# RWKV-7 block of a hybrid trunk: triangular inverse in 32x32 tiles, two chains in flight, tanh in place of sigmoid

## The reference, cut to what matters

```
def wkv_scan(r, w, k, v, a, b, s0, reverse):
    def step(S, xs):
        sa = einsum('bhvk,bhk->bhv', S, a_t)
        S = S * w_t + sa x b_t + v_t x k_t            # x: outer product
        return S, einsum('bhvk,bhk->bhv', S, r_t)

kk = normalised(kf * rw_kk)
for d in (forward, backward):
    w_log = -softplus(-(w0[d] + tanh(x_w) @ w2[d])) - 0.5
    decay = exp(-exp(w_log))                          # = exp(-exp(-0.5) * sigmoid(...))
    a_rate = sigmoid(a0[d] + x_a @ a2[d])
    k_d = kf * (1 + (a_rate - 1) * rw_ka)
    o_d, s_d = wkv_scan(rf, decay, k_d, vf, -kk, kk * a_rate, s0, reverse=d)
```

## Time and profile before

| | |
|---|---|
| median of three runs | 3419.12 us (3416.22 to 3426.52) |
| the profiled execution | 3412.67 us, its span 3410.9 us |
| mean granted TensorE clock | 0.929 of full speed |
| busy, whole span | PE 2957.4 us (87%), PEld 1759.9 (52%), DVE 1448.0 (42%), ACT 564.5 (17%), POOL 377.9 (11%) |
| `block_rwkv` | about 1030 to 1817 us of the span |
| HBM traffic in it | 22 GB/s, against 400 in the experts |

### The profile page before, as it was taken

One profiled execution on the slowest core, in us unless ns is written; L12 is line 12 of the kernel. 1 busy time (PEld: TensorE's weight loads), 2 busy tenths in 40 slices (PEclk: granted clock), 3 DMA queues, 4 the chain that ended last, 5 costly groups with the idle time before them and its releaser, 6 DMA issues. The chain is left out here.

```text
span 3410.9 us, 72845 instructions
## 1 busy us (share of the span) xinstructions
PE 2957.4 (87%) x32237; PEld 1759.9 (52%) x32237; DVE 1448.0 (42%) x2634; ACT 564.5 (17%) x1331; POOL 377.9 (11%) x431
## 2 busy tenths in 40 slices
PE   5899999998595888888884499977999999999993
PEld 1566666665375888888882245442333333323230
DVE  1677577663363665565652311142232232132123
ACT  2100000000352333333332311110000000000001
POOL 0100000000154232322211000000000000000000
PEclk8899999999597999999995799978999999999996
DMA  9565645552451000000005387777999999999997
GB/s 412 195 213 175 208 176 183 208 196 84 143 132 46 24 5 26 26 26 26 25 8 229 138 300 289 276 308 283 395 410 393 412 412 395 399 397 400 408 419 309
DMA packets 224486, 776.86 MB, mean 228 GB/s; under 512 B 55171, under 2 KB 119386, under 8 KB 155635
## 3 DMA queue, kind: packets, MB, share of 16 engines
q1 hardware_dynamic: 212626, 712.26, 54.1%
q0 software_dynamic: 11248, 60.87, 5.9%
q10 hardware_dynamic: 368, 0.10, 0.0%
HBM read 710.98 MB, written 62.18 MB: 227 GB/s over the span
## 5 line engine op out<-in xcount | busy, mean ns | idle before, releaser
L2068 PE MATMUL ex_ps<-experts_ring,ex_xe 128*32 128x512 f32 (+1 forms) x4608 | 674.6, 599 | 49.1 <-DMA experts_ring<-in_w_up 27.6
L2070 PE MATMUL ex_ps<-experts_ring,ex_xe 128*32 128x512 f32 (+1 forms) x1536 | 674.1, 599 | 0.0
L2068 PEld LDWEIGHTS ex_ps<-experts_ring,ex_xe 128*32 128x32 f32 (+1 forms) x4608 | 212.6, 107 | 497.0 <-issue 479.4
L474 DVE SCALAR_TENSOR_TENSOR pj_macc<-pj_mring,head_cond_t,pj_macc 128x1024 f32<-128x1024 f32 x240 | 296.9, 1277 | 184.0 <-DMA pj_mring<-in_w_ada 184.0
L2083 PE MATMUL ex_ps<-experts_ring,ex_hidt 128*32 128x512 f32 (+1 forms) x2304 | 334.3, 594 | 6.9 <-DVE ex_hidt L2150 6.9
L2085 PE MATMUL ex_ps<-experts_ring,ex_hidt 128*32 128x512 f32 (+1 forms) x768 | 333.8, 594 | 0.0
L547 PE MATMUL pj_ps<-head_hT,head_ring_in 128*128 128x320 f32 x1104 | 313.7, 437 | 5.9 <-DVE head_hT L447 3.5
L1866 PE MATMUL om_ps<-experts_ring,om_ot 128*128 128x512 f32 x640 | 287.1, 610 | 15.4 <-DMA om_ot<-scratch_o 15.4
L2172 DVE SCALAR_TENSOR_TENSOR ex_hid<-ex_hid,ex_gcol,ex_ps 80x512 f32<-80x512 f32 x16 | 11.9, 744 | 591.3 <-ACT ex_hid L2115 591.3
L547 PEld LDWEIGHTS pj_ps<-head_hT,head_ring_in 128*128 128x128 f32 x1104 | 211.4, 192 | 96.6 <-DVE head_hT L447 6.3
L2083 PEld LDWEIGHTS ex_ps<-experts_ring,ex_hidt 128*32 128x32 f32 (+1 forms) x2304 | 106.8, 106 | 225.9 <-issue 218.1
(11 more groups left out here) (357 smaller groups left out, 4417.4 us busy)
## 6 DMA issues: line engine op xcount, KB each, us to landing
experts_ring<-in_w_gate SPq DMA_DIRECT2D x128, 1024.0 KB, 21.9
experts_ring<-in_w_up SPq DMA_DIRECT2D x128, 1024.0 KB, 22.6
experts_ring<-in_w_down SPq DMA_DIRECT2D x128, 1024.0 KB, 21.3
experts_ring<-in_w_out SPq DMA_DIRECT2D x68, 1024.0 KB, 6.9
pj_mring<-in_w_ada SPq DMA_DIRECT2D x64, 1024.0 KB, 9.0
head_ring_in<-in_w_in SPq DMA_DIRECT2D x23, 2048.0 KB, 8.0
ada_ring<-in_w_ada SPq DMA_DIRECT2D x16, 2048.0 KB, 19.0
scratch_z<-pj_stage POOLq DMA_DIRECT2D x19, 640.0 KB, 8.2
```

Of the source, the lines that this page charges most:

```text
L474: a = nc.vector.scalar_tensor_tensor(acc, w, scalar, acc, ALU.mult, ALU.add)
L2068: pe.matmul(ps[rows, bank, :], xe[:, k, rows], cols, start=(k == 0), stop=(k == KD - 1))
L2070: mm = pe.matmul(ps[96:96 + rows.stop - rows.start, bank, :], xe[:, k, rows], up[:, g1], start=(k == 0), stop=(k == KD - 1))
```

## The change

It rewrites the order and the inverse inside `block_rwkv` and nothing else.

- The inverse is made only in 32x32 tiles: four levels (blocks of 2 to 16) on the two diagonal 32x32 tiles of each 64x64, that is on the four tiles (0,0), (1,1), (2,2), (3,3) of the array for the two heads, and a fifth level that fills the off-diagonal tile. `tt` has 32 columns; its transpose is no longer made by products (`dt`, `ti` go) but by VectorE's 32x32 transpose (`turn`). Batches are two, of five chunks. The result is spread into `tw` (64 columns) by GpSimd (`spread_own`) and by VectorE at the last level.
- Two chains run at a time, of the two directions, each in its own PSUM banks: in line u the second half of unit u-2's chain is interleaved stage by stage with the first half of unit u-1's. R goes from 6 to 4 banks. The state is scaled by one product with a decay pair that GpSimd forms (`decay_pairs`), in place of two pointer operands.
- Both sigmoids become tanh with scale 0.5 on ScalarE; the "1 +" is added by VectorE ahead of the scan, and `LAM` and the vectors are halved. `bb` = (rate + 1) times kk is formed by VectorE (`removal`) instead of GpSimd.
- The order in a line changes: `sc` first, with `w` and `a` of the next unit between; `bk`, `vt`, `s0` are fillers between the levels. `vt` is done once for a pair and not once for a unit, reads `vt` without ScalarE's copy, and `wa2`, `sin`, `bk` have two buffers. Masks are built for four 32-row groups.

The core of the diff ("..." where lines are left out):

```diff
-    LAM = float(np.exp(-0.5))
-    LEVELS = [2, 4, 8, 16, 32]
-    BATCH = [(0, 4), (4, 7), (7, 10)]
-    R = 6
...
+    LAM = 0.5 * float(np.exp(-0.5))
+    CHAINS = 2
+    R = 4
+    NS = 1 + CHAINS
+    HB, BC = CK // 2, NCK // 2
+    LAST_LV = 4
+    GROUPS = tuple(slice(HB * g, HB * g + HB) for g in range(4))
...
+    def plan(u):
+        fr = front_jobs(u + 1) + [None] * 5
+        vt = [("vt", b, u) for b in range(2)] if u % 2 == 0 else [None] * 2
+        items = [("sc", 0, u), fr[0], ("sc", 1, u), fr[1], ("sc", 2, u), fr[2], ("sc", 3, u), fr[3], ("sc", 4, u)]
+        items += ["scan"] if more else []
+        fill = [("bk", 0, u), ("bk", 1, u), ("bk", 2, u), fr[4], vt[0], vt[1]]
+        for lv in range(LAST_LV + 1):
+            for b in range(2):
+                items += (["turn%d" % b] if lv == 0 else []) + [("x", b, lv, u)]
+            if lv < 3:
+                items.append(fill[2 * lv])
+            if more and lv == 2:
+                items.append("removal")
+            for b in range(2):
+                items.append(("d", b, lv, u))
+                if more and lv == 3:
+                    items.append(("exp_in", "exp_inv")[b])
+                if more and lv == 4:
+                    items += (["pad_b"], ["pad_k", "pad_a"])[b]
+            if lv < 3:
+                items.append(fill[2 * lv + 1])
+            if more and lv == 3:
+                items += ["exp_ex", "decay"]
...
+    def sequence(u):
+        old, new = chain(u - 2, BC, NCK), chain(u - 1, 0, BC)
+        return [s for pair in itertools.zip_longest(old, new) for s in pair if s is not None]
+    COST = {"sc": 9, "w": 6, "a": 6, "s0": 2, "bk": 9, "vt": 6, "x": 7, "d": 7}
...
         @block.gpsimd
-            for i in range(6):
-                n = 2 ** i
-                for rows in HEADS:
+            for i in range(5):
+                n = 2 ** i
+                for rows in GROUPS:
...
+            def start(u, b):
+                n = MADE + 3 * (2 * u + b)
+                pool.wait_ge(dve_ev, RANK[G["sc", (BC * b + BC - 1) // 2, u]])
+                nc.gpsimd.tensor_tensor(part[:], lt, first[:].unsqueeze(1).to_broadcast([P, BC, 2, HB]), ALU.mult).then_inc(tinit, 1)
...
         @block.tensor
-                elif kind == "ti":
-                    pe.wait_ge(tinit, 6 * u + 2 * b + 2)
...
+                    last = key[2] == LAST_LV
+                    for i in range(BC):
+                        c = BC * b + i
+                        out = bank[:, i * HB:(i + 1) * HB]
+                        for g, rows in enumerate(GROUPS):
+                            at = GROUPS[g ^ 1] if last else rows
+                            if kind == "x":
+                                h = (g + 1) % 2 if last else g % 2
+                                lhs, rhs = sc[rows, u % NS, c, 0, HB * h:HB * h + HB], tm[rows, c, :]
+                            else:
+                                lhs, rhs = xm[rows, c, :], tt[rows, c, :]
+                            mm = pe.matmul(out[at], lhs, rhs, start=True, stop=True)
...
         @block.scalar
-                    return nc.scalar.activation(sg[:, cols], bank[:, 0:HALF], ACT.Sigmoid, bias=pp[:, 5 + d:6 + d])
+                    a = nc.scalar.activation(sg[:, cols], bank[:, 0:HALF], ACT.Tanh, scale=0.5, bias=pp[:, 5 + u % 2:6 + u % 2])
...
         @block.vector
-            dve.wait_ge(once_in, 64)
-            dve.wait_ge(made, 2)
+            dve.wait_ge(once_in, 8 * 16)
+            dve.wait_ge(tinit, MADE)
+            def turn(u, b):
+                nc.vector.transpose(chunks(tm, b).rearrange("p c k -> p (c k)"), chunks(tt, b).rearrange("p c k -> p (c k)")).then_inc(turned, 1)
...
+            def scan(v):
+                nc.vector.tensor_scalar(sg[:], sg[:], 1.0, None, ALU.add).then_inc(cs_done, 1)
                 nc.vector.tensor_tensor_scan(cs[:], reset[:], sg[:], 0.0, ALU.mult, ALU.add).then_inc(cs_done, 1)
+            def removal(v):
+                nc.vector.scalar_tensor_tensor(bb[:], ar[:], 1.0, kk[:], ALU.add, ALU.mult).then_inc(cs_done, 1)
```

More of the change, by code:

```diff
@@ L1106, in block_rwkv, with on_act @@
+    LINES = [timeline(u) for u in range(NU + CHAINS)]
+    JOBS = front_jobs(0) + [i for line in LINES for i in line if not isinstance(i, str) and i[0] != "seq"]
+    G = {key: g for g, key in enumerate(JOBS)}
+    def on_act(key):
+        return key[0] in ("w", "a", "s0", "vt", "bk") or key[0:1] + key[2:3] == ("x", LAST_LV)
+    RANK = [sum(on_act(m) == on_act(key) for m in JOBS[:g + 1]) + on_act(key) for g, key in enumerate(JOBS)]
     with ExitStack() as ctx:
@@ L1147, in block_rwkv @@
-        w_done, w_ev, u_done, u_ev, z_done, z_ev, o_ev, s_ready = (sem(n) for n in ("wd", "we", "ud", "ue", "zd", "ze", "oe", "sr"))
-        fs_done, fo_out, osum_done, o_out = sem("fs"), sem("foout"), sem("osum"), sem("oout")
-        block = ctx.enter_context(nc.Block())
-        NLOAD = 10 * 16
-        def periods(period):
-            for p in range(NPAIR):
-                for d in range(2):
-                    period(p, d, first=p + d == 0, last=p == NPAIR - 1 and d == 1)
+        par_ready = sem("parrdy")
@@ new lines, in _ @@
+            pool.wait_ge(once_in, 8 * 16)
+            front(0)
+            scaled_r(0)
+            decay_pairs(0)
+            added = 0
+            for u in range(NU):
+                for b in range(2):
+                    start(u, b)
+                if u + 1 < NU:
+                    front(u + 1)
+                    scaled_r(u + 1)
+                for b in range(2):
+                    spread_own(u, b)
+                if u + 1 < NU:
+                    decay_pairs(u + 1)
+                if u % 2 == 0 and u // 2 >= CHAINS:
+                    add_directions(added)
+                    added += 1
@@ L1366, in stage @@
[L1366 to L1370 removed]
+                        emptied([("x", 1, LAST_LV, v), ("d", 1, LAST_LV, v)])
@@ L1379, in period @@
-            def period(p, d, first, last):
-                for item in timeline:
-                    if item[0] == "job":
-                        run_job(item[1], p, d, first, last)
-                    elif not first:
-                        stage(item[1], item[2], 2 * p + d - 1, 1 - d)
-            pe.wait_ge(loads, NLOAD)
-            for n, (kind, half) in enumerate(FRONT_JOBS):
-                front_job(kind, half, 0, rot[:, n]).then_inc(job, 1)
-            periods(period)
-            for i, s in stages:
-                stage(i, s, 2 * NPAIR - 1, 1)
+                    pe.wait_ge(w_ev[k], q + 1)
@@ L1406, in empty @@
[L1406 to L1418 removed]
+            act.wait_ge(once_in, 8 * 16)
@@ L1483, in _ @@
-            copy_values(0)
-            act.wait_ge(par_ready, 2)
-            for n, (kind, half) in enumerate(FRONT_JOBS):
-                act.wait_ge(job, n + 1)
-                take_front(kind, half, 0, rot[:, n]).then_inc(act_ev, 1)
-            exponentials(0, 0, first=True)
-            periods(period)
-            for i, s in stages:
-                stage(i, s, 2 * NPAIR - 1, 1, NPAIR - 1)
+                    act.wait_ge(u_done[k], q + 1)
+                    nc.scalar.copy(usb[:, k, :], wu[:, k, DH:2 * DH]).then_inc(u_ev[k], 1)
+                else:
+                    act.wait_ge(z_done[k], q + 1)
+                    act.wait_ge(z_ev[k], q + 2)
+                    if i == 0 and v // 2:
+                        act.wait_ge(osum_done, v // 2)
+                    nc.scalar.copy(of[:, v % 4, c * CK:(c + 1) * CK], zo[:, k, DH:2 * DH]).then_inc(o_ev[k], 1)
@@ L1583, in _ @@
-            vectors(0)
-            scan(FRONT)
-            scaled(0, 0, first=True)
-            scaled(1, 0, first=True)
-            scaled_a(0, 0, ready=False)
-            periods(period)
-            for i, s in stages:
-                stage(i, s, 2 * NPAIR - 1, 1)
+                    nx = ORDER[k][i + 1]
+                    nc.vector.tensor_tensor(fs[:, k, :], tmp[:, k, :], ec[:, r, c:c + 1].to_broadcast([P, DH]), ALU.mult)
+                    nc.vector.tensor_tensor(st[:, k, :], s0[:, r, :], ec[:, r, nx:nx + 1].to_broadcast([P, DH]), ALU.mult).then_inc(s_ready[k], 1)
+                elif i + 1 < NCK:
+                    nc.vector.tensor_tensor(st[:, k, :], tmp[:, k, :], ecp[:, r, c:c + 1].to_broadcast([P, DH]), ALU.mult).then_inc(s_ready[k], 1)
```

611 lines of the change are left out of this document (311 added, 300 removed).

## The result

The changed kernel takes 3534.23 us (median of 4 runs, 3525.01 to 3541.05) against 3419.67 for the kernel before (3416.22 to 3426.52): 1.033 times as long, interval 1.030 to 1.036. It is slower, where I had forecast 3383 us, and it lies above my range, too. The profiled execution took 3541.05 us with a span of 3539.3, 128.4 us over that of before.

What follows compares the result with a forecast made beforehand. TensorE and its waits were taken as the bound: a period falls from 45.8 to 43.0 us, fifteen give -42, the start adds 6, so 3377 us profiled and 3383 median, range 3300 to 3480.

Steps and rivals of the forecast that it cites:

- Price of a record: Inverse's 800 records on 32x32 tiles: 11 ns each, 8.8 us a period, ends 5.8 to 23.4.
- issue bound: Rival: inverse's records still cost 29.2 ns, the pace of issue; period 51 us, kernel 3505 us; chance 0.11.
- paced between: Rival: inverse's records cost 22 ns, between 15 and 29.2; period 48.0 us, kernel 3458 us; chance 0.07.
- Change of shape: TensorE switching between 32x32 and other tiles, 36 to 38 times a period: 0.1 us each, 3.7 us, ends 0 and 4.5.
- Gaps: Two new TensorE waits a period: 2.9 us ahead of the first x, 2.5 ahead of the next unit's first sc.
- Chain's waits: Waits for the chain's stage results, some 5 us a period, all go with two chains in flight.
- Clock: Half-clock dips in the recurrence: 1.5 a period at 1.8 us each, 2.7 us, ends 0 and 5.4.
- gaps and clock: Rival: gaps and light load halve the clock for a third of the period, 4 us more; 3443 us; chance 0.10.
- the experts' 15 ns: Spacing of the experts' 32-column products on four tiles, cited against issue bound, though over short bursts only.
- Start: Block start: more mask selects delay VectorE's first instruction, so all starts 6 us later, ends 2 and 8.
- First unit: First unit of the block: saves what it loses in bare gaps.
- Tail: Last chain work at the block's end, five rounds of two and five of one: change 0, within 4 us either way.

Runs made afterwards that it cites:

- e10: Changed kernel with the inverse on 64x64 tiles and gaps filled with needed work, but one chain in flight instead of two: 3371 us, ratio 0.989 to before.
- e7: Changed kernel with one chain in flight instead of two, 32x32 tiles and tanh kept: 3596 us, ratio 1.053 to before.
- e6: Changed kernel with the inverse on 64x64 tiles, two bk jobs ahead of the first x, pads ahead of the last d: 3315 us, ratio 0.971 to before.
- e1: Changed kernel with five unused wide products put in front of the first x and first sc of every unit but the first: 3493 us, ratio 1.025 to before.
- e5: Changed kernel in its own order with the inverse's products on two 64x64 tiles instead of four 32x32: 3450 us, ratio 1.010 to before.
- e8: Changed kernel with five bare product streams ahead of the recurrence, run once for its trace: first 32x32 stream 27.9 ns a record, with holes every 128.
- e12: Changed kernel with other bare and mixed streams ahead of the recurrence, run once for its trace: 64x64 tiles with 32 columns took 29.1 ns a record.

## Why the prediction was wrong

Step by step, for one period; the ledger of the changed kernel is 12.5 + 4.4 + 3.4 (wide products, as forecast) + 7.0 + 5.0 + 5.8 + 4.6 = 42.7, and 10.6 us are left for clock and restarts.

- *Price of a record*: 11 ns forecast, 8.7 measured, -1.8 us. The step I held for the most uncertain came out in my favour, and both rivals built on it, issue bound and paced between, were wrong for the record itself. The Trainium skill, TensorE: Matmul & The Clock Gate, Part 1, states a floor of about 25 ns from start to start, however small the product. The runs show both sides of it: on 64x64 tiles 32 columns cost 27.7 ns, close to it, on four 32x32 tiles 8.7, far below.
- *Change of shape*: 0.1 us forecast, 0.14 measured, 5.0 us for 3.7: +1.3, beyond my upper end of 4.5. That the record and the change together come to 12.0 us where I had 12.5 is two errors that cancel, and luck.
- *Gaps*: 2.9 and 2.5 us forecast, 2.91 and 2.68 in the period shown, 5.8 in the mean: right.
- *Chain's waits*: gone but for 0.5 us a period, right. e10 shows that the second chain does it once the clock is up; at the pace of the changed kernel one chain shows few of them too (e7).
- *Clock*: the step that failed. I had put "1.5 dips in each period, 2.7 us", each dip with the size of one in the kernel before, 1.8 us. There were 2.8 in each period, with 23.7 us of half clock. The clock's 0.78 over 53.3 us is up to 11.7 us; the ledger gives 8.9. (In e6 it leaves 38.6 - 12.5 - 4.4 - 3.4 - 11.6 - 3.8 = 2.9 us, of which its clock of 0.97 takes 1.2 and restarts 1.7; 1.7 of the 10.6 above are restarts too.) The number and the depth per dip both failed. Behind the first gap, where narrow products and one `bk` job stand, a dip lasts 3.4 us in 11 of 14 periods, as before. Behind the holes it lasts 6.8 us or more, but for one. Behind the second gap, on wide products, it lasts up to 16 us, and in seven periods of fourteen nearly all of that stretch. Filling this gap took the half clock there from 9.4 to 0.1 us a period (e1), so the gap is its cause; why it then lasts so long on wide products, when a dip in the kernel before is over in 3.6 us, stays open. The rival "gaps and clock" had the mechanism, but gave it 4 us where 6 to 9 were due.
- *Supply of instructions*: a term that is missing, 4.6 us, and a third dip of the clock with it. My sum priced a record by how fast the array takes it and asked nowhere how fast 1306 of them (so many has the trace; the 1336 in the expectation of e5 are too many) with their loads arrive in 43 us. At 27.9 ns a record they need 36.4, so the mean was no bound; but little is held in store for bursts, and the stretches of `x` and `d` run through 128 records in 2.4 us. I had 29.2 ns as "the pace of issue" in a rival and let it fall with the experts' 15 ns, a burst of a few records that could not show it.
- *Start*: VectorE's first instruction came 9.7 us later, of which 5.2 were there when the block began (its first GpSimd instruction at 1035.49 against 1030.32; where they come from is not shown): 4.5, for a forecast of 6.
- *First unit*: "saves what it loses in bare gaps" was wrong: from VectorE's first instruction to the first clearing 68.6 us against 47.1, +21.5, at a clock of 0.56 from its first `sc` on where before had 0.92 from its first `bk` on. In that stretch TensorE stands 13.5 us, 7.0 of them for issue, where before it stood 1.7; the rest fits with half clock, which again holds through the wide `sc` and low-rank products at the start.
- *Tail*: 32.5 us against 34.7, within the 4 either way.

Together: 5.2 + 4.5 + 21.5 + 96.5 - 2.2 = 125.5 us. The two failed terms are 14 x (4.6 + 6.2) = 151 us, if the clock's 8.9 stand against the 2.7 I gave it: without them a period is 42.5 us, near my 43.0. e6, with 400 records fewer and work in the gaps, removes nearly all of both, and its period is 38.6.

## What to carry to other kernels

Count a stretch's instructions as well as its columns: where products are so small that 128 of them, loads included, take much less than the 3.6 us in which the next 128 come, the rest is standing time, and the saving is lost. Two gaps of 2.7 us cost twice, once as time and once as clock, and the second cost can be the larger: the half clock behind one of them lasted up to 16 us, on wide products. So put independent work into a wait; here it gave back the clock even where the work was of no use. When one stage is made faster, don't take the number and the length of the clock's dips from the old kernel: price a stretch behind a new gap at both levels of the clock, and let the range hold both.

## What the runs showed of the hardware that was not expected

- TensorE stands after every 128 records (loads included, one 16.4 KB packet of the instruction queue) when they are consumed faster than one block in about 3.6 us: 27.9 ns a record in the bare stream of e8, 29.5 in the mixed one of e12. A hole ends 2.4 to 2.8 us behind the packet.
- A record of 32 columns on a 64x64 tile costs 27.7 to 29.1 ns at 2.4 GHz, about as much as one of 64 columns (29.2), and 53 ns at 1.2 GHz; on four 32x32 tiles in turn 8.5 to 8.7 and 13 ns. A change between the two shapes costs 0.14 us.
- A stream of 64x64 tiles with 32 columns kept the clock that it began with: 1.00 for 28 us in e12, 0.50 for 51 us in e8. A stream with holes of 0.4 to 1.1 us stayed at 1.00, two with holes of 1.1 to 2.5 us fell to 0.50.
- Wide work does not always bring the clock back soon: behind a gap of 2.7 us TensorE ran 64 to 320 columns wide products at 0.50 for up to 16 us, hardly standing (the changed kernel, 1274 to 1290 us). With five products of no use in that gap the half clock there was 0.1 us a period for 9.4 (e1).
